# Expert lists of a one-layer decoder kernel: scattered records read back on ScalarE's queue, in place of rank comparisons and index matmuls

## What is computed

```python
def hier_moe(h, w_rg, b_rg, w_re, b_re, w_gate, w_up, w_down):
...
    gprob = jax.nn.softmax((x @ w_rg + b_rg).astype(jnp.float32), axis=-1)
    gp, gidx = lax.top_k(gprob, 1)
...
    ep, eidx = lax.top_k(jax.nn.softmax(elog_sel, axis=-1), EXPERT_TOP_K)
    ep = ep / jnp.sum(ep, axis=-1, keepdims=True)
    weights = gp * ep
    expert_id = gidx * EXPERTS_PER_GROUP + eidx
...
        y = (jax.nn.silu(x @ wg) * (x @ wu)) @ wd
        return acc + c[:, None] * y.astype(jnp.float32), None
```

## Time and profile before

| what | value |
|---|---|
| runs | 874.66, 875.93 and 876.08 us, median 875.93 us |
| the profiled execution | 879.06 us, of which the span of the engines' work is 877.3 us |
| TensorE | busy 848.1 us, 97% |
| VectorE, ScalarE, GpSimd | busy 527.4, 383.7 and 243.4 us |
| stage of the experts | from 429.8 us to the end |

### The profile page before, as it was taken

One profiled execution on the slowest core, in us unless ns is written; L12 is line 12 of the kernel. 1 busy time (PEld: TensorE's weight loads), 2 busy tenths in 40 slices (PEclk: granted clock), 3 DMA queues, 4 the chain that ended last, 5 costly groups with the idle time before them and its releaser, 6 DMA issues.

```text
span 877.3 us, 15841 instructions
## 1 busy us (share of the span) xinstructions
PE 848.1 (97%) x5828; PEld 752.3 (86%) x5828; DVE 527.4 (60%) x1237; ACT 383.7 (44%) x734; POOL 243.4 (28%) x272
## 2 busy tenths in 40 slices
PE   8999999999999999997899999999999999999993
PEld 7999879999988787774789998889988999888992
DVE  5627424667878335557585666646666656766573
ACT  7645204556457325444334434344443444433442
POOL 1000000000000200001054655446535556445472
PEclk9999999999999899999699999999999999999997
DMA  9121001102223272336288888987889988898871
GB/s 301 34 96 49 1 5 44 50 1 56 49 96 96 91 243 97 145 145 216 61 299 289 299 291 315 325 300 269 288 306 328 306 287 279 290 359 297 283 258 50
DMA packets 118505, 166.56 MB, mean 190 GB/s; under 512 B 17012, under 2 KB 95928, under 8 KB 118469
## 3 DMA queue, kind: packets, MB, share of 16 engines
q1 hardware_dynamic: 103109, 135.48, 45.8%
q0 software_dynamic: 15360, 30.59, 10.2%
HBM read 146.84 MB, written 41.17 MB: 214 GB/s over the span
## 4 chain that ended last, share of the span: by engine, by line
PE 41%; issue 3%; POOL 3%; DVE 2%; DMA 2%; ACT 1%; another core or an unknown queue 1%; POOLq 0%; DVEq 0%; ACTq 0%
PE bank L1940 27%; PE bank L1950 3%; PE bank L1961 3%; PE bank L1952 3%; PE bank L1951 3%; DMA out<-ot,lists_now 2%; PE bank L1928 1%; POOL out L1848 1%; POOL hold_at L1864 1%; PE bank L1921 1%; POOL big L1835 0%; POOL sums L1848 0%; ACT split L2040 0%; DVE big L2078 0%
## 5 line engine op out<-in xcount | busy, mean ns | idle before, releaser
L1940 PE MATMUL bank<-big,ring 128*128 128x160 f32 x2048 | 286.4, 301 | 1.3 <-DVE x L2216 1.2
L1940 PEld LDWEIGHTS bank<-big,ring 128*128 128x128 f32 x2048 | 282.2, 191 | 2.7 <-DVE x L2216 1.3
L1864 POOL TENSOR_TENSOR hold_at<-ident 128x1 f32<-128x1 f32 x63 | 52.7, 836 | 177.9 <-DVE lists L2111 128.8
L2144 DVE TENSOR_TENSOR wdlo<-wdn,split 128x1024 fp32r<-128x1024 f32 x64 | 76.6, 1218 | 0.0
L2036 ACT ACTIVATE sg<-bank 128x160 f32<-128x160 f32 x64 | 19.5, 304 | 108.1 <-PE bank L1940 93.6
L2040 ACT CAST split<-wdn 128x1024 fp32r<-128x1024 f32 x64 | 64.9, 1039 | 0.0
L504 PE MATMUL bank<-split,ring_r 128*128 128x384 f32 (+1 forms) x192 | 64.4, 336 | 0.1
L506 PE MATMUL bank<-split,ring_r 128*128 128x384 f32 (+1 forms) x192 | 61.7, 321 | 0.0
L2139 DVE TENSOR_TENSOR hs<-hid,hs 128x128 fp32r<-128x128 f32 x64 | 18.8, 294 | 56.6 <-ACT hs L2042 47.5
L1950 PE MATMUL bank<-split,hs 128*128 128x512 f32 x128 | 52.6, 411 | 0.0
L1427 PE MATMUL bank<-split,ring_r 128*128 128x512 f32 (+1 forms) x128 | 51.7, 404 | 0.3 <-PEq L1219 0.3
(11 more groups left out here) (390 smaller groups left out, 1794.2 us busy)
## 6 DMA issues: line engine op xcount, KB each, us to landing
wdn<-in_w_down SPq DMA_DIRECT2D x32, 1024.0 KB
ring<-in_w_gate SPq DMA_DIRECT2D x32, 1024.0 KB, 5.5
ring<-in_w_up SPq DMA_DIRECT2D x32, 1024.0 KB
ring<-in_w_in SPq DMA_DIRECT2D x8, 1024.0 KB, 5.9
x<-in_x_prompt SPq DMA_DIRECT2D x8, 512.0 KB, 6.4
h_rows<-h SPq DMA_DIRECT2D x8, 512.0 KB, 2.6
sums<-x SPq DMA_DIRECT2D x8, 512.0 KB, 3.6
v<-in_x_prompt SPq DMA_DIRECT2D x4, 512.0 KB, 5.0
```

What stands on the lines that cost most here:

```text
L1864: nc.gpsimd.tensor_tensor(hold_at[:], ident[:, 0:1], ident[:, 1:2], ALU.add).then_inc(e_hold, 1)
L1940: x = nc.tensor.matmul(bank[f % 2][:, side * 256:side * 256 + W], ring[:, u, k, c0:c0 + P], xT[:, k, :], start=k == 0, stop=k == KC - 1)
L2144: nc.vector.tensor_tensor(wdlo[:, k, :], wdn[:, k // 2, (k % 2) * D:(k % 2 + 1) * D], wdhi[:, k, :].bitcast(F32), ALU.subtract).then_inc(e ...
```

## The change

- Lists of steps 0 to 6 are made as before, but the comparison reads `rank_m` with fixed columns (no lowering, no copy of the facts), and the steps that make them (0 to 4) are written out instead of looped, on TensorE and VectorE. The weight columns of `table` are filled for 7 experts instead of 16.
- Lists of later steps come from DRAM. A buffer `records` has 114 groups of 160 rows of 8 floats. In the second stage it is filled with blanks by one DMA. VectorE works out, for every token and each of its two experts, the row number (`places_of`, behind step 0) and the record itself (`records_of`, behind step 1). GpSimd writes them with 18 indirect DMAs of 128 records of 32 bytes, six each behind its own steps 1, 2 and 3.
- From step 5 on ScalarE issues, at the head of each step, five DMAs that read the group of step i+2 into `listed`; ahead of the first it waits for all 18 scatters (`e_sent`). VectorE makes the lists from `listed` in three short operations (`next_list`). TensorE has no index matmuls in steps 5 to 14, and VectorE no comparison in steps 4 to 14.

```diff
+        def records_out(tiles):
+            for t in tiles:
+                for a in range(2):
+                    nc.gpsimd.indirect_dma_start(
+                        out=places.records, in_=record[:, a, t, :], in_offset=None, bounds_check=GROUPS * W - 1,
+                        out_offset=bass.IndirectOffsetOnAxis(ap=row_at[:, a, t:t + 1], axis=0),
+                        oob_is_err=False).then_inc(e_sent, 16)
...
+        step(0)
+        step(1)
+        pool.wait_ge(e_record, 1)
+        records_out(range(0, 3))
+        step(2)
+        records_out(range(3, 6))
+        step(3)
+        records_out(range(6, TT))
+        with pool.Fori(4, n - 1) as i:
+            step(i)
...
-                pe.wait_ge(e_oh, i + 3)
-                pe.wait_ge(e_idx, i + 2)
-                indices(facts)
+                if early is not None:
+                    pe.wait_ge(e_oh, early + 3)
+                    pe.wait_ge(e_idx, early + 2)
+                    indices(table[:, early + 2, :, :])
                 pe.wait_ge(e_xg, i * 16 + 32)
                 rows_in(i * 16 + 32)
...
+        def load_list(i):
+            act.wait_ge(e_idx, i + 2)
+            group_rows = places.records[0:GROUPS * W, :].rearrange("(s r) c -> s r c", r=W)[bass.ds(i + 2, 1), :, :]
+            nc.scalar.dma_start(listed[:, 0, :], group_rows[:, 0:P, :].rearrange("o r c -> (o r) c")).then_inc(e_list, 16)
+            for j in range(4):
+                nc.scalar.dma_start(listed[j * W2:(j + 1) * W2, 1, :],
+                                    group_rows[:, P:W, :].rearrange("o r c -> (o r) c")).then_inc(e_list, 16)
...
-        with act.Fori(0, n - 1) as i:
+        act.sem_inc(e_list, 80 * (LISTED - 3))
+        with act.Fori(0, LISTED - 2) as i:
+            step(i, False)
+        act.wait_ge(e_sent, 16 * 2 * TT)
+        with act.Fori(LISTED - 2, n - 1) as i:
+            load_list(i)
             step(i, False)
...
+        def places_of():
+            ranks = rank_m[:].rearrange("p (e t) -> p t e", e=NE)
+            for a in range(2):
+                m = weighing.picks[:, a, :, :]
+                nc.vector.tensor_tensor(chosen[:, a, :, :], m, ranks, ALU.mult)
+                x = nc.vector.tensor_tensor(chosen[:, 2 + a, :, :], m, places.start[:].unsqueeze(1).broadcast_to([P, TT, NE]),
+                                            ALU.mult)
+            link(x)
+            link(nc.vector.tensor_reduce(group[:], chosen[:], axis=AX.X, op=ALU.add))
...
+        def next_list(i):
+
+            dve.wait_ge(e_list, i * 80)
+            nc.vector.tensor_copy(lists[:, :, 0], listed[:, 0, 0:4])
+            nc.vector.tensor_copy(weight[:], listed[:, :, 4])
+            nc.vector.scalar_tensor_tensor(out=lists[:, :, 1], in0=listed[:, 1, 0:4], scalar=4.0,
+                                           in1=chunk[:].broadcast_to([P, 4]), op0=ALU.mult, op1=ALU.add).then_inc(e_idx, 1)
...
-                dve.wait_ge(e_ix, i + 3)
-                indices(i + 2)
-                dve.wait_ge(e_rk, i + 3)
-                onehot((i + 3) % NE)
-                dve.wait_ge(e_oh, i + 4)
-                lower((i + 3) % NE)
+                if early is not None:
+                    dve.wait_ge(e_ix, early + 3)
+                    indices(early + 2)
+                    if early + 3 < LISTED:
+                        onehot(early + 3)
+                else:
+                    next_list(i)
...
-        step(0, True, False)
-        with dve.Fori(1, n - 1) as i:
+        step(0, True, False, 0)
+        places_of()
+        step(1, False, False, 1)
+        records_of()
+        for i in range(2, LISTED - 2):
+            step(i, False, False, i)
+        with dve.Fori(LISTED - 2, n - 1) as i:
             step(i, False, False)
```

More of the change, by code:

```diff
@@ L1223, in b2_all @@
 def b2_all(nc, A, O, S0, Sp, s_w, samples, halves, sb, sem, e_w, wdn, bank, ident, onesf, eps_c, uT, gT, ring, x1, x_rows, h2_dram,
-           sums_dram, rank_m, table, iota_w, steps, once, weighing, rows_0):
+           sums_dram, rank_m, table, iota_w, steps, once, weighing, rows_0, places):
     c2 = ExitStack()
@@ L1720, in _ @@
         link(nc.vector.tensor_tensor(s2, w1, s2, ALU.mult))
[L1721 to L1724, removed]
+        rest, second = [pr.rearrange("p t g j -> p (t g j)")[:, LISTED * TT * j:LISTED * TT * (j + 1)].rearrange("p (e t) -> p e t", e=LISTED)
+                        for j in range(2)]
+        for out, m, w in ((rest, M1, w1), (second, M2, s2)):
+            link(nc.vector.tensor_tensor(out, m.rearrange("p t e -> p e t")[:, 0:LISTED, :],
+                                         w.unsqueeze(1).broadcast_to([P, LISTED, TT]), ALU.mult))
+        link(nc.vector.tensor_tensor(rest, rest, second, ALU.add))
         for part in (2, 3, 4):
-            link(nc.vector.tensor_copy(table[:, :, :, part], rest))
+            link(nc.vector.tensor_copy(table[:, 0:LISTED, :, part], rest))
             if part < 4:
-                link(nc.vector.tensor_tensor(rest, rest, table[:, :, :, part], ALU.subtract))
+                link(nc.vector.tensor_tensor(rest, rest, table[:, 0:LISTED, :, part], ALU.subtract))
     block.close()
@@ L1968, in left_sums, with step @@
                              start=True, stop=True).then_inc(e_ms, 1)
-        def step(i, first, last):
+        def step(i, first, last, early=None):
             pe.wait_ge(e_xe, i * 3 + 3)
@@ L2010, in _ @@
         indices(table[:, 0, :, :])
-        step(0, True, False)
+        step(0, True, False, 0)
         pe.wait_ge(e_same, 3)
-        with pe.Fori(1, n - 1) as i:
+        for i in range(1, LISTED - 2):
+            step(i, False, False, i)
+        with pe.Fori(LISTED - 2, n - 1) as i:
             step(i, False, False)
@@ L2164, in third_table, with step @@
         def third_table():
-            dve.wait_ge(e_rk, 2)
             onehot(2)
-            dve.wait_ge(e_oh, 3)
-            lower(2)
             dve.wait_ge(e_g, 80)
-        def step(i, first, last):
+        def step(i, first, last, early=None):
             if first:
```

108 lines of the change are left out of this document (84 added, 24 removed).

## The result

The changed kernel takes **894.64 us** (median of 4 runs, 893.81 to 895.62) against 875.36 us for the kernel before beside it (874.66 to 876.08): ratio 1.0217, 95% interval 1.0198 to 1.0236, or 19.3 us more. The forecast was 884.2 in a range up to 889.5. The sign was right, the size was not, and the time lies outside the range. The profiled execution took 895.21 us, its span is 893.4.

What follows compares the result with a forecast made beforehand. The prediction took TensorE's matmuls to bound each expert step. Its terms, -4.3 + 7.3 + 2.9 + 0.9 + 1.5 = +8.3 us on 875.9, gave 884.2 us, range 873 to 889.5.

Steps and rivals of the forecast that it cites:

- Index products, -4.3: TensorE, steps 5 to 14: index matmuls gone, 0.44 us each in the chain, nearly all counting, -4.3 us.
- Five issues on ScalarE, +7.3: Head of steps 6 to 14: issues take 2.67 us, slack 1.86, TensorE waits 0.81 at f = 2; +7.3 us (0 to 19).
- rival of short issues: ScalarE's five issues take under 1.86 us, so steps 6 to 14 lose nothing; 874.7 us; chance 0.28.
- `places_of`, +0.9: VectorE behind step 0: 3.6 us of work makes block 0's `hid` late for f = 2; +0.9 us (0.3 to 2).
- `records_of`, nothing: VectorE: eleven operations, about 1.9 us, free before 547.3, so no cost.
- GpSimd's batches, +1.5 (0 to 6): Six scatters behind each of GpSimd's steps 1 to 3: next fetch 2.2 us later, 0.5 a batch, +1.5 us.
- slack of f = 1: TensorE's block f = 1 waits for the sums of the step before, which end 1.96 us before it begins.
- First list load, +2.9: Step 5: ScalarE waits 2.1 us for all 18 scatters; with issues, less slack, loses +2.9 us (0.8 to 6).
- Written-out steps, nothing: Expert steps written out instead of looped: more code but no work, so no cost.
- rival of a DMA bound: Small reads and writes fill the DMA engines' idle time, weights for f = 2 come late; 889 us; chance 0.10.

## Why the prediction was right in sign and wrong in size

- **Index products, -4.3.** Right: 0.51 us a step, ten steps, -5.1. They just fit, as reckoned from the fourth `hid`.
- **Five issues on ScalarE, +7.3.** Right, and for the reason given. The five took 2.44 us (2.67 taken from the earlier trace rows), TensorE lost 0.89 us in each of nine steps, 8.0 in all; alone on the kernel before +8.2. The 50 ns of the Trainium skill, "DMA: Bandwidth & Descriptors", would have made this term zero; but its section "Anatomy of one DMA" gives them for the path of DMAs that GpSimd issues, and the prediction took them over to ScalarE's queue. Here an issue took 0.34 to 0.58 us. The rival of short issues is refuted.
- **`places_of`, +0.9, and `records_of`, nothing.** `places_of` was sized at 3.6 us of VectorE, measured 463.13 to 466.35, 3.2. It cost 0.36 us in step 1. `records_of` took the forecast's 1.9 us, but did not fit: VectorE was late in step 2, and TensorE waited 0.67 us at f = 2 for the `hid` behind it. Step 2 took 29.2 us, 2.4 more. About half of that is not from `records_of`: the kernel before with nothing but written-out steps took 28.04 there, with a wait of 1.11 us for the sums as here of 1.30. These 2.4 us I had at nothing; why the results land late there stays open.
- **GpSimd's batches, +1.5 (0 to 6).** This is the step that failed: "2.2 us later ... the slack of f = 1 is 1.96 ... I take 0.5 a batch". Measured +20.8 for the scatters alone. The idle time and the slack were read rightly. Wrong was to stop at the fetch, with scatters at their lone pace. The lateness was 8.5 us: the batch with its hold 10.4 us long beside the comparison, landings up to 4 us slower, and then the clock. The upper bound of 6 us for all three batches was passed by the first one alone: in the kernel before with the scatters added, step 4 took 10.8 us more.
- **First list load, +2.9.** ScalarE did wait for the scatters in step 5, TensorE stood 3.06 us at f = 2. But the third batch, for which ScalarE waited, ended 10.9 us into step 5 (585.52) and not 2.3 as forecast (568.6), since GpSimd was late by the second; what the wait cost alone stays open.
- **Written-out steps, nothing.** Right where they stand alone (+1.1, at the edge of what can be told), wrong as a rule: with scatters ahead of the landing wait 15 to 17 us. In the changed kernel itself this is 3.2 us at most (894.6 against 891.4 with the loop).
- **The clock.** In no term; 5.8 us in steps 4 and 5.

The rival of a DMA bound had the right sign and came nearer in time (889), but batches of three move the same packets for 1.6 us. Together, against steps of 26.84: steps 6 to 14 took 3.4 more (8.0 for the issues less 4.6 for nine index products), steps 1 and 2 took 2.7 more, steps 4 and 5 took 16.1 more, from batches, first load and clock. That is 22.2. In the two profiles step 1 begins 1.4 us earlier in the changed kernel (457.58 against 458.99), and what follows step 14 is 1.6 us shorter (37.8 against 39.4), which leaves the 19.3 measured. Why these two are shorter was not looked for.

## What to carry to other kernels

Work put into the idle time of an engine off the critical path was free here up to about 7.8 us a batch, and above that mostly cost many times what stuck out: follow the lateness through every landing and hold to the engine that waits, with the pace that the added work has beside its neighbours, and add the clock behind each standstill. Put it where the engine waits anyway (here ahead of a wait for a landing: 24 us less than behind it on the kernel before with TensorE in a loop, but nothing gained with TensorE's steps written out), or in pieces that fit. And issues at the head of a step are worth counting: fewer DMAs with a repeated source did as well as another queue.

## What the runs showed of the hardware

- A scatter of 128 rows takes GpSimd 0.98 us, beside VectorE's comparison 2.3 to 3.1. The Trainium skill, "SBUF — State Buffer", section "SBUF: two separate sides", tells of a port pair that VectorE and GpSimd hold in turn for a whole instruction; the trace agrees: in the changed kernel the long scatter began 0.7 us behind the comparison (511.00 and 510.30) and ended 0.85 us behind it (513.70 and 512.85), about the time of a lone scatter.
- The wait for the two stores of sums was 1.29, 2.52, 4.02 and 5.62 us in different steps and versions. The longest was the one whose second store began with SyncE's weights.
- TensorE's steps written out, and scatters on GpSimd ahead of its landing wait, each nearly free (+1.1 and -3.2 us), cost 13.9 us together on the kernel before.
- After standstills of TensorE of 2 to 7 us the granted clock was 0.73 to 0.88 over the next 6 to 15 us.
- The versions of the kernel before with added scatters had steps of 26.76 us in place of 26.84. Why was not looked for.
